# Hidden activations of a feed-forward, transposed by VectorE and moved by DMA, in place of TensorE's transposes

## The reference

```python
D_MODEL, SEQ, DEPTH = 1024, 256, 2
D_FF = 2816

def ffn_sublayer(x, norm_pre, w_gate, w_up, w_down, norm_post):
    h = rms_norm(x, norm_pre)
    y = (jax.nn.silu(h @ w_gate) * (h @ w_up)) @ w_down
    return rms_norm(y, norm_post)

def reference(x, ...):
    h = x
    for l in range(DEPTH):
        h = h + mixer_sublayer(h, ...)
        h = h + ffn_sublayer(h, ffn_norm_pre[l], w_gate[l], w_up[l], w_down[l], ffn_norm_post[l])
    return h
```

## Time and profile before

| | |
|---|---|
| median of 3 runs | 804.21 us (804.03 to 804.45) |
| the profiled execution | 804.11 us, of which the trace spans 802.3 us |
| granted TensorE clock | 0.998 of full speed (the upper level, 2.4 GHz) |
| TensorE busy | 794.7 us, 99% |
| VectorE, ScalarE, GpSimd busy | 556.8 us (69%), 427.5 us (53%), 78.7 us (10%) |
| moved by DMA | 145.47 MB, 181 GB/s |

### The profile page before, as it was taken

How to read it: one execution, slowest core, us unless ns; L and a number is a source line. 1 busy time by engine, 2 the same in 40 slices (tenths; PEclk the granted TensorE clock), 3 DMA queues, 4 the chain that set the end, 5 groups by cost and what they waited for, 6 DMA issues and landing times.

```text
span 802.3 us, 10124 instructions
## 1 busy us (share of the span) xinstructions
PE 794.7 (99%) x3828; PEld 671.7 (84%) x3828; DVE 556.8 (69%) x790; ACT 427.5 (53%) x604; POOL 78.7 (10%) x111
## 2 busy tenths in 40 slices
PE   9999999999999999999999999999999999999997
PEld 7998888888888888888889888888888888888885
DVE  6689999789674555554476979996877655555443
ACT  6587555554554444444475666565536544445431
POOL 1620000122300000000221100002304000000000
PEclk9999999999999999999999999999999999999999
DMA  9675444445575556555355644444563755555531
GB/s 358 220 251 172 146 153 152 157 153 189 178 245 192 184 177 203 168 197 188 129 199 191 214 158 145 144 158 157 167 226 132 259 186 185 183 183 165 205 129 52
DMA packets 41487, 145.47 MB, mean 181 GB/s; under 512 B 4656, under 2 KB 4656, under 8 KB 41440
## 3 DMA queue, kind: packets, MB, share of 16 engines
q1 hardware_dynamic: 41040, 143.15, 52.9%
q0 software_dynamic: 256, 1.16, 0.4%
q10 hardware_dynamic: 144, 0.52, 0.2%
HBM read 143.77 MB, written 1.05 MB: 181 GB/s over the span
## 4 chain that ended last, share of the span: by engine, by line
PE 98%; DMA 1%; ACT 0%; DVE 0%; DVEq 0%; POOLq 0%; issue 0%; SPq 0%; POOL 0%; ACTq 0%
PE acc L397 28%; PE acc L399 27%; PE acc L398 27%; PE acc L516 7%; PE tp L471 4%; PE misc L678 1%; PE tp L696 1%; PE tp L483 1%; DMA gates<-x_cols 1%; PE misc L638 0%; PE tp L654 0%; PE misc L397 0%; PE misc L399 0%; PE misc L398 0%; PE misc L640 0%; ACT w_hi L830 0%
## 5 line engine op out<-in xcount | busy, mean ns | idle before, releaser
L1156 DVE TENSOR_TENSOR w_lo<-raw,w_hi 128x1024 fp32r<-128x1024 f32 (+2 forms) x246 | 300.6, 1229 | 153.4 <-ACT w_hi L830 151.7
L830 ACT ACTIVATE w_hi<-raw 128x1024 fp32r<-128x1024 f32 (+2 forms) x252 | 259.8, 1041 | 197.5 <-PE acc L399 191.3
L397 PE MATMUL acc<-w_hi,xT_hi 128*128 128x512 f32 (+2 forms) x692 | 269.2, 389 | 0.0
L399 PE MATMUL acc<-w_hi,xT_lo 128*128 128x512 f32 (+2 forms) x692 | 265.2, 383 | 0.0
L398 PE MATMUL acc<-w_lo,xT_hi 128*128 128x512 f32 (+2 forms) x692 | 265.0, 383 | 0.0
L399 PEld LDWEIGHTS acc<-w_hi,xT_lo 128*128 128x128 f32 x692 | 129.9, 188 | 24.8
L398 PEld LDWEIGHTS acc<-w_lo,xT_hi 128*128 128x128 f32 x692 | 130.1, 188 | 23.5
L397 PEld LDWEIGHTS acc<-w_hi,xT_hi 128*128 128x128 f32 x692 | 130.1, 188 | 23.4
L397 PE MATMUL acc<-w_hi,hT_hi 128*128 128x512 f32 (+1 forms) x300 | 117.6, 392 | 0.0
L399 PE MATMUL acc<-w_hi,hT_lo 128*128 128x512 f32 (+1 forms) x300 | 116.3, 388 | 0.0
L398 PE MATMUL acc<-w_lo,hT_hi 128*128 128x512 f32 (+1 forms) x300 | 116.2, 387 | 0.0
(11 more groups left out here) (146 smaller groups left out, 631.9 us busy)
## 6 DMA issues: line engine op xcount, KB each, us to landing
raw<-weights SPq DMA_DIRECT2D x247, 512.0 KB, 3.4
raw<-weights SPq DMA_DIRECT2D x14, 384.0 KB, 3.5
raw<-weights SPq DMA_DIRECT2D x8, 288.0 KB, 3.9
gain<-gains SPq DMA_DIRECT2D x4, 512.0 KB, 6.8
x_sb<-x_rows SPq DMA_DIRECT2D x2, 512.0 KB, 9.4
out_rows<-x_sb SPq DMA_DIRECT2D x4, 256.0 KB, 2.1
const<-consts POOLq DMA_DIRECT2D x1, 896.0 KB, 7.9
gates<-x_cols SPq DMA_DIRECT2D x3, 256.0 KB, 7.5
```

The source lines that it names most:

```text
L397: pe.matmul(out, a_hi, b_hi, start=start, stop=False)
L399: return pe.matmul(out, a_lo, b_hi, start=False, stop=stop)
L830: ins = act.activation(w_hi[:, s, first:end], raw[:, s, first:end], ACT.Copy, scale=by)
L1156: ins = dve.tensor_tensor(w_lo[:, s, 0:width], raw[:, s, 0:width], f(w_hi[:, s, 0:width]), ALU.subtract)
```

## The change

The hidden columns are no longer transposed by TensorE. VectorE, right after it has computed a chunk of hidden columns, transposes each 32x32 block of it in place of the block's own (`turn`, one instruction for each token tile, from `hid` to `turned`). A block then has features on partitions, but lies in the quadrant (32 partitions) of its tokens; DMAs bring it into the quadrant of its features. `place` issues, on GpSimd's queue, 16 DMAs for a chunk, one for each pair of quadrants: 32 partitions, two token tiles, 128 floats (512 B) each, from `turned` to `placed`, both of them areas in `gates`. Then ScalarE copies the rounded values to `hT_hi` (`hi_hidden`) and VectorE subtracts (`lo_hidden`). The semaphores are `turn_done` (VectorE to GpSimd, and for reuse of `hid`), `place_in` (all 16 DMAs of a chunk), `hid_hi` and `hid_lo` (to TensorE, ahead of each fourth unit of the down projection).

The places in the order move too. The parts of chunk j-1 are taken after the conversions of units 8j+8 and 8j+9 of the feed-forward instead of before them; those of chunk 4 after unit 120 instead of 114, those of chunk 5 (the last 256 columns) after unit 127 instead of 118. The twelve uses of the `tp` banks by hidden columns are gone from the list `TP`.

```diff
@@ semaphores, tiles and helpers
+BLK = 32
+QUADS = P // BLK
+        turned, placed = (gates[:, i, 0:D].rearrange("p (q t k j) -> p q t k j", q=QUADS, t=TOK, k=4)
+                          for i in range(2))
+        def hid_tiles(j):
+            return slice(4 * j, min(4 * j + 4, FT))
+        def placed_for(j, t):
+            k = hid_tiles(j)
+            return placed[:, :, t, 0:k.stop - k.start, :].rearrange("p q k j -> p k q j")
+        def hid_part(dst, j, t):
+            return dst[:, hid_tiles(j), tokens(t)].rearrange("p k (q j) -> p k q j", q=QUADS)
@@ TensorE
                 for j in range(1, FULL_CHUNKS):
                     col_group(U_FFN + 8 * j, 4, 2, 512, 0, f"F{j}", XT)
-                    hid_transposes(f"H{2 * (j - 1)}", f"F{j - 1}", 4, 2)
                     col_group(U_FFN + 8 * j + 4, 4, 2, 512, 1, f"F{j}", XT)
-                col_group(U_LAST, 4, 2, 2 * LAST_W, 0, "FL", XT, beside=last_beside)
+                col_group(U_LAST, 4, 2, 2 * LAST_W, 0, "FL", XT)
                 def down_waits(i, t):
-                    if i == 2 and t == 0:
-                        hid_transposes("HL0", "FL", 2, 0)
                     if i % 4 == 0:
-                        tp_emptied(pe, l, TPN["H0"] + i // 2 + t)
+                        pe.wait_ge(hid_lo, TOK * (l * CHUNKS + i // 4) + t + 1)
@@ ScalarE
+                def hi_hidden(j):
+                    act.wait_ge(place_in, 16 * QUADS * QUADS * (l * CHUNKS + j + 1))
+                    for t in range(TOK):
+                        act.activation(hid_part(hT_hi, j, t), placed_for(j, t), ACT.Copy).then_inc(hid_hi, 1)
...
-                    for t in range(TOK):
-                        hi_T(f"H{2 * (j - 1) + t}", hT_hi[:, 4 * (j - 1):4 * j, tokens(t)])
-                    his(U_FFN + 8 * j + 8, U_FFN + 8 * j + 12)
+                    his(U_FFN + 8 * j + 8, U_FFN + 8 * j + 10)
+                    hi_hidden(j - 1)
+                    his(U_FFN + 8 * j + 10, U_FFN + 8 * j + 12)
...
                 act.preload_act_table(ACT.Sigmoid)
-                his(117, 119)
-                for t in range(TOK):
-                    hi_T(f"HL{t}", hT_hi[:, FT - 2:FT, tokens(t)])
-                his(119, 135)
+                his(117, 121)
+                hi_hidden(4)
+                his(121, 128)
+                hi_hidden(5)
+                his(128, 135)
@@ VectorE
+                def turn(j, b):
+                    tiles = hid_tiles(j).stop - 4 * j
+                    if l or j:
+                        dve.wait_ge(place_in, 16 * QUADS * QUADS * (l * CHUNKS + j))
+                    for t in range(TOK):
+                        dve.wait_ge(free[b + t], l * FREED[b // 2] + freed(b // 2, f"F{j}" if j < 5 else "FL") + 1)
+                        dve.transpose(turned[:, :, t, 0:tiles, :].rearrange("p q k j -> p k q j"),
+                                      hid[:, t, 0:tiles * P].rearrange("p (k q j) -> p k q j", k=tiles, q=QUADS)
+                                      ).then_inc(turn_done, 1)
+                def lo_hidden(j):
+                    for t in range(TOK):
+                        dve.wait_ge(hid_hi, TOK * (l * CHUNKS + j) + t + 1)
+                        dve.tensor_tensor(hid_part(hT_lo, j, t), placed_for(j, t), f(hid_part(hT_hi, j, t)),
+                                          ALU.subtract).then_inc(hid_lo, 1)
...
                 for t in range(TOK):
                     hidden(t, "F0")
+                turn(0, 2)
                 for j in range(1, FULL_CHUNKS):
                     los(U_FFN + 8 * j + 4, U_FFN + 8 * j + 8)
-                    for t in range(TOK):
-                        k = slice(4 * (j - 1), 4 * j)
-                        lo_T(f"H{2 * (j - 1) + t}", hT_lo[:, k, tokens(t)], hT_hi[:, k, tokens(t)])
-                    los(U_FFN + 8 * j + 8, U_FFN + 8 * j + 12)
+                    los(U_FFN + 8 * j + 8, U_FFN + 8 * j + 10)
+                    lo_hidden(j - 1)
+                    los(U_FFN + 8 * j + 10, U_FFN + 8 * j + 12)
                     for t in range(TOK):
                         hidden(t, f"F{j}")
+                    turn(j, 2)
...
-                los(117, 119)
...
-                los(119, 135)
+                los(117, 121)
+                turn(5, 0)
+                lo_hidden(4)
+                los(121, 128)
+                lo_hidden(5)
+                los(128, 135)
@@ GpSimd, at the end of each layer's program: place(l, j) for j in 0 to 5
+            def place(l, j):
+                pool.wait_ge(turn_done, TOK * (l * CHUNKS + j + 1))
+                if l or j:
+                    pool.wait_ge(hid_lo, TOK * (l * CHUNKS + j))
+                width = (hid_tiles(j).stop - 4 * j) * BLK
+                for q in range(QUADS):
+                    for c in range(QUADS):
+                        src, dst = (gates[BLK * at:BLK * (at + 1), i, D // QUADS * to:D // QUADS * (to + 1)]
+                                    .rearrange("p (t n) -> p t n", t=TOK)[:, :, 0:width]
+                                    for i, at, to in ((0, q, c), (1, c, q)))
+                        pool.dma_start(dst, src).then_inc(place_in, 16)
```

More of the change, by code:

```diff
@@ L42 @@
 LAST_W = D_FF - 512 * FULL_CHUNKS
+CHUNKS = FULL_CHUNKS + 1
+BLK = 32
+QUADS = P // BLK
 POOL_LO = {(l, u) for l in range(LAYERS) for u in (U_FFN, U_FFN + 1)}
@@ L88 @@
        "MT0", "MT1", *(f"{piece}{n}" for n in range(8) for piece in "PV"), "O0", "O1",
-       "M0", "M1", "M2", "M3", "F0", "F1", "F2", "F3"] + [f"H{i}" for i in range(10)] + ["HL0", "HL1"])
+       "M0", "M1", "M2", "M3", "F0", "F1", "F2", "F3"])
 TPN = {name: n for n, name in enumerate(TP)}
@@ L254, in build @@
         last_silu = sem("last_silu")
+        turn_done = sem("turn_done")
+        place_in = sem("place_in")
+        hid_hi = sem("hid_hi")
+        hid_lo = sem("hid_lo")
         half_sq = sem("half_sq")
@@ L784, in _ @@
                 col_group(U_FFN + 4, 4, 2, 512, 1, "F0", XT, begun=1)
-                def hid_transposes(name, chunk, tiles, bank):
-                    for t in range(TOK):
-                        acc_freed(pe, l, bank + t, chunk)
-                        transposes(TPN[name] + t, [(hid[:, t, c * P:(c + 1) * P], P) for c in range(tiles)])
                 for j in range(1, FULL_CHUNKS):
                     col_group(U_FFN + 8 * j, 4, 2, 512, 0, f"F{j}", XT)
-                    hid_transposes(f"H{2 * (j - 1)}", f"F{j - 1}", 4, 2)
                     col_group(U_FFN + 8 * j + 4, 4, 2, 512, 1, f"F{j}", XT)
-                def last_beside(i):
-                    if i == 2:
-                        hid_transposes("H8", "F4", 4, 2)
-                col_group(U_LAST, 4, 2, 2 * LAST_W, 0, "FL", XT, beside=last_beside)
+                col_group(U_LAST, 4, 2, 2 * LAST_W, 0, "FL", XT)
                 def down_waits(i, t):
-                    if i == 2 and t == 0:
-                        hid_transposes("HL0", "FL", 2, 0)
                     if i % 4 == 0:
-                        tp_emptied(pe, l, TPN["H0"] + i // 2 + t)
+                        pe.wait_ge(hid_lo, TOK * (l * CHUNKS + i // 4) + t + 1)
                 wide_group(U_DOWN, FT, "DOWN", HT, down_waits,
@@ L1084, in _ @@
                                        ).then_inc(free[t], 1)
-                    for t in range(TOK):
-                        hi_T(f"H{2 * (j - 1) + t}", hT_hi[:, 4 * (j - 1):4 * j, tokens(t)])
-                    his(U_FFN + 8 * j + 8, U_FFN + 8 * j + 12)
-                his(113, 115)
-                for t in range(TOK):
-                    hi_T(f"H{8 + t}", hT_hi[:, FT - 6:FT - 2, tokens(t)])
-                his(115, 117)
+                    his(U_FFN + 8 * j + 8, U_FFN + 8 * j + 10)
+                    hi_hidden(j - 1)
+                    his(U_FFN + 8 * j + 10, U_FFN + 8 * j + 12)
+                his(113, 117)
                 for t in range(TOK):
@@ L1446, in _ @@
                 los(74, 81)
+                def turn(j, b):
[12 more added lines that the diff above has]
+                                          ALU.subtract).then_inc(hid_lo, 1)
                 def hidden(t, use):
                     bank(2 + t, use)
+                    if l or use != "F0":
+                        dve.wait_ge(turn_done, TOK * (l * CHUNKS + int(use[1])))
                     acc_freed(dve, l, t, use)
@@ L1457, in _ @@
                     hidden(t, "F0")
+                turn(0, 2)
                 for j in range(1, FULL_CHUNKS):
                     los(U_FFN + 8 * j + 4, U_FFN + 8 * j + 8)
-                    for t in range(TOK):
-                        k = slice(4 * (j - 1), 4 * j)
-                        lo_T(f"H{2 * (j - 1) + t}", hT_lo[:, k, tokens(t)], hT_hi[:, k, tokens(t)])
-                    los(U_FFN + 8 * j + 8, U_FFN + 8 * j + 12)
+                    los(U_FFN + 8 * j + 8, U_FFN + 8 * j + 10)
+                    lo_hidden(j - 1)
+                    los(U_FFN + 8 * j + 10, U_FFN + 8 * j + 12)
                     for t in range(TOK):
                         hidden(t, f"F{j}")
```

(11 more changed lines are left out.)

## The result

| | median | runs |
|---|---|---|
| before | 804.03 us | 803.94 to 804.45 |
| after | 795.98 us | 795.75 to 796.10 |

The ratio is 0.9898, with a 95% interval from 0.9883 to 0.9912: 8.05 us faster, where 10.0 were forecast. The profiled execution of after took 795.79 us, its span is 794.0, against 804.11 and 802.3 before: 8.3 us less by the spans. All times here are of fast runs; one run of the kernel with one early drain took 1328.96 us at a granted clock of 0.557 and is in no median.

What follows compares the result with a forecast made beforehand. TensorE, busy 794.7 of 802.3 us, was taken to bound the kernel; 804.11 less 10.0 us of transposes gives 794.1, plus 0.1 for the median 794.2 us, all other work hidden. Range 793 to 807.

Steps and rivals of the forecast that it cites:

- TensorE's time (10.0 us): 88 hidden transposes leave TensorE, all on the path: 9.9 to 10.1 us by the rows, taken as 10.0 us off.
- ScalarE and VectorE: Copies and subtractions now read SBUF, VectorE gains 24 block transposes; VectorE 13.7 us of a 21.75 us chunk, no bound.
- The placing: GpSimd's 16 DMAs per chunk land just about when ScalarE comes for them; unseen up to 12.4 to 12.8 us.
- c: Time of one GpSimd placing issue, taken as 0.57 us; rows gave 0.53 to 0.81.
- L: Time from the turn's end until a chunk is placed: 15 c + 3.9, 12.5 us at c = 0.57.
- The limits beyond it: TensorE stalls over L = 20.9 us; turns run late over 14.2; a layer's stall is L + 3 (L - 14.2) - 20.9.
- The constant of a round: Work behind late copies until the next turn ends, conversions to signals: 7.5 us, added to L and set against 21.75.
- The break-even: Where stalls eat the whole gain: 5.0 us a layer, at L = 17.1, c = 0.88; slower from there.
- Rival 1: GpSimd's issues are held by VectorE's subtractions: c = 0.96, L = 18.3, stall 9.7 us a layer, 813.6 us; chance 0.10.
- Rival 2: Engines pace the 16 small transfers: c 0.83 to 1.2, stall 2 to 24 us a layer, 798 to 842; upper part 0.13.
- Rival 3: No change: a wait of about the transposes' length replaces them on TensorE, c near 0.88, 804 us; chance 0.03.
- The sum (794.2): Whole kernel: profiled 804.11 less 10.0 gives 794.1, the median of runs 0.1 above it: 794.2 us.

Runs made afterwards that it cites:

- one early drain: Against the changed kernel, GpSimd drains its queue once after issuing the last placing of the last layer; 794.19 us.
- the old order: Against the changed kernel, parts of hidden chunks 0 to 3 are taken ahead of converting units 8j+8 and 8j+9 again, on ScalarE and VectorE; 796.21 us.
- one column: Against the kernel with a drain in each layer, GpSimd clears one column and waits for itself ahead of each placing issue; 797.37 us.

## Why the prediction was right, and where it was not

**TensorE's time (10.0 us).** Right: 10.24 by the two chains, 9.93 by putting the transposes back.

**ScalarE and VectorE.** Right. A pair of turns took 1.29 us, for which 1.3 was taken from a row of another instruction of the same size; twice that is hidden too.

**The placing.** I took c = 0.57, L = 12.5 and a free allowance of 12.4 to 12.8 us. The issues took 0.498 us. L can be read where ScalarE waits for it: in the old order it is 11.1 to 11.4 us in five chunks of eight (from the turn's end at 307.08 to the copies at 318.19 in the row shown), 12.9 and 12.7 in two and 14.2 behind the late batch, and with the turn done twice 12.0 to 12.8. So L is not one number, and the 12.5 lies within its spread. The allowance was exact: the copies come 12.4 us after the turn (319.05 - 306.62), and in after ScalarE waited once, 1.8 us, behind the late batch. The limits beyond it, which the profile of before alone gave, held within some 2 us a layer where they were tried: 1.5 us a layer were lost at L = 16.6 (the mean of the first four chunks with one column), where they give 2.8, and 12.3 at 19.2, where they give 13.1. The constant of a round was 7.0, not 7.5. The break-even, 5 us a layer, was not tried itself; on a line between those two points it lies at L = 17.4, and it was put at 17.1. For the last chunks of a layer the estimate was too generous: nothing was to come from there for c under 1.2, and at c = 0.90 TensorE waits 0.6 us a layer for the hidden product of the last columns.

**Rival 1 (issues held by VectorE).** False: VectorE works more than half of the time of a batch, and of 192 issues the longest took 0.63 us. The Trainium skill (SBUF — State Buffer, "Who interferes with whom") infers that two-input instructions of VectorE don't starve GpSimd's descriptors; these rows agree for the subtractions of the weights, which run under the issues. Of block transposes they show nothing: GpSimd's batch waits for the turns, and none of the 24 turns lies under an issue. **Rival 2 (transfers pace themselves).** False: the placing has 2.8% - 0.4% of 16 engines' time for 6144 packets, 0.05 us each, 32 on an engine in a chunk instead of 80: 1.6 us where 2.5 was taken. **Rival 3** false.

**The sum (794.2).** It was 1.8 us too low, and the step that failed is the one on GpSimd's other work: it asked only what GpSimd does between the batches, not what its queue does at the end of the program. The sum carried the tail of before unchanged. The term left out is the closing drain, 5.90 us instead of 1.00, of which 4.1 lie under the output's last store. With that moved, the time is 794.19, the forecast.

## What to carry to other kernels

When one engine is busy 99%, price each of its instructions by the distance of its neighbours' starts, and then look for the other engines' deadlines: how late may the new work be before the ring is empty, and does lateness add up from round to round? Those two sums came out of the profile of before and held within some 2 us a layer up to L = 19.2; at 26.05, where the end of the layer came in, they were 16 us short. And follow a queue that gets new work to the end of the program: what it has to settle there is paid in the open, unless it is settled earlier under cover.

## What the runs showed that was not expected

GpSimd's DMA queue behaves as if it kept a record of each DMA that a drain settles at 0.082 us: closing drains of 0.66, 1.00, 8.51 and 8.85 us with 0, 4, 96 and 100 DMAs since the last drain, whether the youngest were 40 us old (96) or 400 (100). The 5.90 us of the changed kernel fits 64, those issued since the pause. That pause, ahead of the 133rd DMA, stands in all three kernels that issue all DMAs without a drain after the first layer (after, one early drain, the old order), and in none that has that drain. In after it made the batch 3.1 us late. That it settles the records of before is inferred from the 5.90 us and from the kernel with a drain after the first layer, where both forecasts of that idea (no pause, 8.5 us at the end) came out. At 0.082 us those 132 would have taken 10.8 us; where the rest of that lay (the queue idled for 17.0 us before that batch) was not tried.

A block transpose of 128x512 float32 on VectorE takes 0.67 us, as long as its subtraction of that size (0.68). An issue of GpSimd for 32 KB between two places in SBUF takes 0.50 us, and such a transfer lands 1.7 to 4.6 us after its issue, 3.4 in the median. Eight transposes of 128x128 in a stream of 128x512 matmuls cost TensorE 0.9 us, 0.11 each, where the instruction's own row says 0.27.
